# A two-block transformer kernel: the order of the tiles in the last feed-forward round before the second mixer

## The reference

```python
f_lat = sqrelu_mlp(modulate(h_lat, g_pre_ff[0], ml[3], ml[4]), w_ff1[0], w_ff2[0])
h_lat = h_lat + ml[5] * rms_norm_2(f_lat, g_post_ff[0])
f_ctx = sqrelu_mlp(modulate(h_ctx, g_pre_ff[0], mc[3], mc[4]), w_ff1[0], w_ff2[0])
h_ctx = h_ctx + mc[5] * rms_norm_2(f_ctx, g_post_ff[0])
...
u_lat = modulate(h_lat, g_pre_mix[1], ml[0], ml[1])      # layer 1
u_ctx = modulate(h_ctx, g_pre_mix[1], mc[0], mc[1])
p_ctx, p_lat = u_ctx @ w_in, u_lat @ w_in                # odd_mixer
```

## Time and profile before

| | us |
|---|---|
| median of 3 runs | 2056.38 |
| lowest and highest | 2055.04, 2061.04 |
| the profiled execution | 2060.76 |
| its span | 2058.9 |
| the last round's start to the first latent product of `proj1_k` | 63.84 |

### The profile page before, as it was taken

The page is one execution under the profiler, slowest core; times in us unless marked ns, Lnnn a source line. Parts: engine busy times, 40 slices in busy tenths (PEclk is TensorE's granted clock), DMA queues, the critical chain, the costliest instruction groups (busy, mean ns, idle before and its releaser), DMA issues. The chain is left out here.

```text
span 2058.9 us, 36819 instructions
## 1 busy us (share of the span) xinstructions
PE 1926.6 (94%) x15696; PEld 1615.2 (78%) x15696; DVE 1132.2 (55%) x1798; ACT 863.8 (42%) x1531; POOL 210.3 (10%) x249
## 2 busy tenths in 40 slices
PE   7998999899899999989999998999999879888998
PEld 5756998685699978856898987888877678677987
DVE  6554775465567655466556665544444545536643
ACT  5353664345456543445322334322222243545532
POOL 1100221020012200101113311000000101000000
PEclk9987999999799999999999999999999989998999
DMA  7682665458456552335000032333323214014653
GB/s 261 203 307 83 187 184 192 141 177 307 142 144 185 178 169 86 99 109 183 3 24 4 4 124 62 114 110 95 113 84 100 62 63 138 25 43 134 190 186 123
DMA packets 231641, 264.53 MB, mean 128 GB/s; under 512 B 14214, under 2 KB 153782, under 8 KB 231095
## 3 DMA queue, kind: packets, MB, share of 16 engines
q1 hardware_dynamic: 230891, 261.36, 40.1%
q10 hardware_dynamic: 588, 0.82, 0.1%
HBM read 261.07 MB, written 1.09 MB: 127 GB/s over the span
## 5 line engine op out<-in xcount | busy, mean ns | idle before, releaser
L401 PE MATMUL acc<-rounded,rounded 128*128 128x512 f32 (+1 forms) x2552 | 883.8, 346 | 24.7 <-DVE rounded L653 11.0
L402 PE MATMUL acc<-rounded,rounded 128*128 128x512 f32 (+1 forms) x2552 | 874.9, 343 | 0.0
L403 PE MATMUL acc<-rounded,rounded 128*128 128x512 f32 (+1 forms) x2552 | 874.1, 342 | 0.0
L385 DVE TENSOR_TENSOR rounded<-arena,rounded 128x2048 fp32r<-128x2048 f32 (+1 forms) x194 | 434.2, 2242 | 299.4 <-ACT rounded L374 299.3
L401 PEld LDWEIGHTS acc<-rounded,rounded 128*128 128x128 f32 x2552 | 488.0, 191 | 93.8 <-issue 20.5
L402 PEld LDWEIGHTS acc<-rounded,rounded 128*128 128x128 f32 x2552 | 488.1, 191 | 60.4 <-issue 1.9
L403 PEld LDWEIGHTS acc<-rounded,rounded 128*128 128x128 f32 x2552 | 487.5, 191 | 60.4
L374 ACT ACTIVATE rounded<-arena 128x2048 fp32r<-128x2048 f32 (+1 forms) x194 | 363.0, 1874 | 349.4 <-PE acc L403 308.4
L1406 DVE SCALAR_TENSOR_TENSOR arena<-acc,pcol,arena 128x254 f32<-128x254 f32 (+1 forms) x176 | 76.8, 478 | 52.3 <-ACT arena L1387 50.8
L823 PEld LDWEIGHTS sc<-arena 128*128 128x128 f32 x592 | 72.8, 196 | 37.9 <-ACT arena L929 20.4
L1990 PE MATMUL sc<-arena 64*64 64x64 f32 x2560 | 95.6, 224 | 6.9 <-DVE arena L2140 5.8
(11 more groups left out here) (243 smaller groups left out, 1691.8 us busy)
## 6 DMA issues: line engine op xcount, KB each, us to landing
arena<-in_w_ff SPq DMA_DIRECT2D x64, 1024.0 KB, 5.3
arena<-in_w_ada SPq DMA_DIRECT2D x48, 1024.0 KB, 5.2
arena<-in_w_up SPq DMA_DIRECT2D x88, 512.0 KB, 5.1
arena<-in_w_in SPq DMA_DIRECT2D x24, 1024.0 KB, 5.2
arena<-in_w_down SPq DMA_DIRECT2D x20, 1024.0 KB, 5.1
arena<-in_w_out SPq DMA_DIRECT2D x16, 1024.0 KB, 5.1
arena<-in_w_in_even SPq DMA_DIRECT2D x9, 1024.0 KB, 5.4
arena<-in_w_in_odd SPq DMA_DIRECT2D x8, 1024.0 KB, 5.3
```

What stands on the lines that cost most here:

```text
L385: dve.tensor_tensor(r32(w), w, r32(high_slot(c)[:, 0:size(c)]), ALU.subtract).then_inc(split_made, 1)
L401: pe.matmul(ps, ah, bh, start=first, stop=False)
L402: pe.matmul(ps, ah, bl, start=False, stop=False)
L403: return pe.matmul(ps, al, bh, start=False, stop=last)
```

## The change

The last round gets an order of its own, in the list `CONTEXT_FIRST` of (half, tile): (0, 0), (0, 1), (1, 0), (1, 1), (0, 2), (0, 3), (1, 2), (1, 3). So both halves of the two context tiles come first. `last_round` on PE, `add_last` on DVE and `round_squares` on ACT follow it.

- PE: the four small products stand ahead of the first four accumulators. Context tile 0 is transposed ahead of accumulator 6 (half 1 of tile 2), context tile 1 ahead of accumulator 7. In `proj1_k` both latent tiles are transposed ahead of context product 3.
- The second tile of both norms goes to the "sc" banks instead of "tr" (`TWO_POOLS`).
- DVE: the gate products of half 0 come after accumulators 1 (context) and 5 (latent); context tiles are finished after accumulators 2 and 3; `norm_scale` of context tile 0 after accumulator 4, of tile 1 after 5; `norm_low` of tile 0 after 5, of tile 1 after 6, ahead of the finish of latent tile 2. The split of the second `proj1_k` chunk moves from the middle of the round to its end, on DVE and ACT.
- ACT: `norm_high` of the context tiles moves in between the squares of accumulators 5, 6 and 7.
- The first weight chunk of the round is released after accumulator 6 instead of 4. The scratch of ACT's squares moves from `uT[1]`, which the norm now fills meanwhile, to a free part of `hid[1]`.
- POOL makes the second context tile's 1/rms ahead of the latent tiles' steps.

```diff
@@ plan
+            if e == EIGHTHS - 1:
+                release[-2] = (acc_full, acc_at[("ff2", e)] + 6)
...
+        CONTEXT_FIRST = [(0, 0), (0, 1), (1, 0), (1, 1), (0, 2), (0, 3), (1, 2), (1, 3)]
+        stage("near", sc=8)
         plan_norm(("mix", 1, 1))
         plan_norm(("mix", 1, 0))
-        stage("near", sc=8)
...
         def norm_fill(key, tt, half):
-            return tr_at[("norm", key)] + 2 * tt + half
+            if key in TWO_POOLS and tt:
+                return TWO_POOLS[key], {"acc": acc_at, "sc": sc_at}[TWO_POOLS[key]][("norm", key)] + half
+            return "tr", tr_at[("norm", key)] + 2 * tt + half
@@ DVE, in place of add_round's last round
+            def add_last(self, dve, key, following):
+                self.gate_wait(dve)
+                for n, (hf, t) in enumerate(self.order):
+                    if n < 4:
+                        near_dve(dve, 1, n)
+                    f = acc_at[key] + n
+                    o = self.o[:, t, hf * 512:(hf + 1) * 512]
+                    dve.tensor_tensor(o, o, filled(dve, "acc", f)[:, :], ALU.add).then_inc(drain("acc", f), 1)
+                    if n == 4:
+                        near_used(dve)
+                        norm_scale(dve, following, 0)
+                    if n in (1, 5):
+                        for x in (t - 1, t):
+                            self.squared(dve, 0, x)
+                            self.gate_half(dve, 0, x)
+                    if n == 5:
+                        norm_scale(dve, following, 1)
+                        for half in range(2):
+                            norm_low(dve, following, 0, half)
+                    if n == 6:
+                        for half in range(2):
+                            norm_low(dve, following, 1, half)
+                    if hf:
+                        self.finish(dve, t)
+                ahead_dve(dve, chunk_at[key] + HIGH)
@@ ACT, round_squares
-                tok_walk(act, ahead_act, last, ET, 2, squares, last=False)
+                for n, (hf, t) in enumerate(self.order):
+                    if n in (4, 5):
+                        norm_square(act, following, n - 4)
+                    wait_drained(act, "acc", acc_at[last] + n)
+                    cols = slice(hf * 512, (hf + 1) * 512)
+                    self.square(act, hf, t, self.o[:, t, cols], self.squares[:, t, :])
+                    if n == 5:
+                        norm_high(act, following, 0)
+                    if n == 6:
+                        norm_high(act, following, 1)
+                ahead_act(act, chunk_at[last] + HIGH)
@@ PE
-                    if block == 1 and n == 3 and key == ("ff2", EIGHTHS - 1):
-                        norm_turn(pe, ("mix", 1, 1), 0)
+            def last_round(key, lhsT):
+                for n, (hf, t) in enumerate(CONTEXT_FIRST):
+                    if n < 4:
+                        near_pe(pe, 1, n)
+                    if n >= 6:
+                        norm_turn(pe, ("mix", 1, 1), n - 6)
+                    w = parts(pe, chunk_at[key] + hf)
+                    ps = claim(pe, "acc", acc_at[key] + n)
+                    for k in range(ET):
+                        ins = mm3(pe, ps[:, :], lhsT(k, t), both(w, lambda v: v[:, k, :]), k == 0, k == ET - 1)
+                    ins.then_inc(acc_full, 1)
...
-            norm_turn(pe, ("mix", 1, 1), 1)
-            feat_gemm_by_stream(pe, "proj1_k", PK, 4, lambda s: ("mix", 1, s), {2: 0, 3: 1})
+            feat_gemm_by_stream(pe, "proj1_k", PK, 4, lambda s: ("mix", 1, s), {3: [0, 1]})
@@ POOL, post_pool
-                if norms and t >= 2:
+                if norms and t >= 2 and not (context_first and t == 3):
                     norm_pool(pool, tiles[t - 2][0], [tiles[t - 2][1]])
+                if context_first and t == 2:
+                    norm_pool(pool, *[(key, [tt]) for key, tt in tiles][1])
                 post.pool_rstd(pool, t)
```

More of the change, by code:

```diff
@@ L663, in norm_dve @@
                     norm_scale(dve, norm, 0)
-                if not norm[4]:
+                early = not norm[4] and norm[0] not in TWO_POOLS
+                if early:
                     norm_low(dve, norm, 0, 0)
@@ L669, in norm_dve @@
                     for half in range(2):
-                        if norm[4] or tt or half:
+                        if not early or tt or half:
                             norm_low(dve, norm, tt, half)
@@ L723, in feat_gemm_by_stream @@
                 for i in range(n):
[L724 to L725 removed]
+                    for tt in turns.get(i, ()) if s else ():
+                        norm_turn(pe, norm(0), tt)
                     w = parts(pe, chunk_at[key] + i // 2)
@@ L2371, in __init__ @@
                 self.ss, self.ms, self.rs = stats(2 * n), stats(n), stats(n)
+                self.order = CONTEXT_FIRST if key == "ff0" else [(hf, t) for hf in range(2) for t in range(n)]
                 self.rows_before = sum(len(p.streams) for p in posts.values())
```

91 lines of the change are left out of this document (40 added, 51 removed).

## The result

| | before | after |
|---|---|---|
| median of 20 runs each | 2059.05 | 2047.00 |
| lowest and highest | 2055.01, 2064.53 | 2041.76, 2060.84 |
| the profiled execution, its span | 2060.76, 2058.9 | 2041.76, 2039.9 |
| the last round's start | 1613.09 | 1607.18 |
| from there to the first latent product of `proj1_k` | 63.84 | 50.88 |

After to before is 0.9948, 95% interval 0.9936 to 0.9959: some 10.7 us faster, with 8.4 to 13.2 us in the interval. The ratio is not that of the two medians, which differ by 12.05 us. The forecast was 2043.6, range 2039.5 to 2050.0.

What follows compares the result with a forecast made beforehand. TensorE, busy 94%, was taken as the bound, waiting 8.0, 5.8 and 3.5 us for VectorE's serial chain. Work 42.2, waits 8.5 and joints 0.3 gave 51.0 against 63.84 us, so 2056.38 - 12.8 = 2043.6 us, range 2039.5 to 2050.0.

Steps and rivals of the forecast that it cites:

- The walk: Last round's start to proj1_k's first latent product, followed instruction by instruction: 51.0 us against 63.84, 12.8 less; chance 0.55.
- the slow 7.52 us of products 0 and 1: Context products 0 and 1 of proj1_k charged at the fallen clock, after a forecast wait of 3.4 us.
- The 'sc' banks are long empty, which takes away the 5.8 us.: Ahead of context tile 1's transposes: the 5.8 us wait for an emptied "tr" bank goes.
- Context product 2 waits 1.6 us for it.: In proj1_k: TensorE waits 1.6 us for the second chunk's split, now behind both latent tiles on VectorE.
- What lies behind moves as a whole.: Behind the first latent product: nothing changes length, the 2.64 us wait stays, changed releases cost nothing.
- the last gap of the stretch: Rival: clock also falls in the 2.6 us wait ahead of the first latent product, costing 1.8 us, 2045.4 us; chance 0.15.
- The queue: Rival: VectorE's queue from 1628 to 1664 is longer than walked, gain 8 us, 2048.4 us; chance 0.12.
- The waits did not shrink further: Rival: the 1.6 and part of the 2.6 and 3.4 us waits go, gain 16 us, 2040.4 us; chance 0.07.
- Slow from the first wait on: Rival: clock stays low from the first wait to the projections' end, 12.6 us slower, 2069.0 us; chance 0.03.
- Taken back behind: Rival: a wait behind proj1_k, a load in first place, swallows the gain, 2052 to 2058 us; chance 0.08.
- A gain in the stretch that the span does not show: Sign of a wrong forecast: round start to first latent product gets shorter, the whole execution does not.
- The base: Starting median of the whole kernel, 2056.38 us from three runs, minus 12.8 gives 2043.6 us.

Runs made afterwards that it cites:

- one_pool: Changed kernel with both tiles of each norm transposed through the "tr" banks again, no "sc" banks: ratio to before 0.9946, round start to first latent product 50.86 us.
- lows_last: Changed kernel with both context tiles' low and high parts behind the finish of all four tiles again: ratio to before 0.9989, round start to first latent product 56.66 us.
- old_tile_order: Changed kernel with the old tile order and context update, scale and transpose places; pools and late split kept: ratio to before 1.0017, round start to first latent product 60.19 us.
- filler: Changed kernel with 20 spare matmuls on TensorE ahead of context product 0 of proj1_k: ratio to before 0.9974, round start to first latent product 53.40 us.
- latent_scaled_first: Changed kernel with latent tile 0 scaled ahead of the second chunk's split, tile 1 behind it, latent transposes apart: ratio to before 0.9951, stretch 49.66 us.
- before_again: The kernel before, unedited, run once more for its trace: median 2055.33 us, round start to first latent product 64.04 us.
- split_mid: Changed kernel with the second proj1_k chunk's split moved between the two latent tiles: ratio to before 0.9953, round start to first latent product 49.76 us.
- combined: Changed kernel with split between latent tiles, latent transposes apart, latent tile 0 scaled between latent updates, tile 1 inside tile 0's low parts: ratio to before 0.9917, stretch 48.04 us.
- after_again: The changed kernel, unedited, run once more: median 2049.49 us, ratio to before 0.9949, round start to first latent product 50.87 us.

## Why the prediction was right, and where it was not

**The walk.** Forecast and measured, counted from the round's start:

| | forecast | measured |
|---|---|---|
| first transposes (wait) | 21.1 (0.9) | 21.12 (0.78) |
| first product of `proj1_k` (wait) | 31.9 (3.4) | 31.56 (2.87) |
| products 0 and 1 | 7.52 | 7.43 |
| context product 2 (wait) | 41.0 (1.6) | 40.70 (1.71) |
| first latent product (wait) | 51.0 (2.6) | 50.88 (2.50) |

No start is off by more than 0.4 us and no wait by more than 0.53. Following the chain through VectorE instruction by instruction was what made this possible: sums of TensorE's waits would not have given it, as one_pool shows. lows_last and old_tile_order came out within the stretches expected of them by the same kind of walk. One term of the sum was right in size and free in effect: the slow 7.52 us of products 0 and 1. filler made them fast, and product 2 started 40.72 us behind the round's start all the same.

**"The 'sc' banks are long empty, which takes away the 5.8 us."** Right that the wait goes, wrong why: one_pool has no second pool and the same stretch. The prediction's own walk had already put the gain of context tile 0 ahead of the latent tiles; the pool then had nothing left to free.

**"Context product 2 waits 1.6 us for it."** The wait was forecast to 0.1 us, and it was a cost, as the prediction had it: moving the split brought 1.1 us. The walk took 0.3 us for GpSimd's adds, and the one beside the split took 1.95. That this did no harm was not foreseen: tile 0 waited for product 2 in any case. In latent_scaled_first, where it does not, a slow add of this kind cost 0.87 us.

**"What lies behind moves as a whole."** The 2.64 us wait was there and no load or release came late. But of three traces of after two have a tail 3 us longer at a lower clock; lows_last and old_tile_order 10 and 13.5 us. This is the step that failed, in part. The ratio gives 10.7 us where the stretch gives 13.0; a tail that is 3 us longer in most executions of after and in few of before would make up the difference. That is argued: two and three traces can't set how often, and the interval of the ratio (8.4 to 13.2 us) holds the 13.0 as well, so that the medians don't show that anything is missing.

**The rivals.** The clock did not fall in the last gap of the stretch in any trace of after (2.50 us). The Trainium skill (TensorE: Matmul & The Clock Gate, "HAM oscillation") tells of a clock that falls in every wait between bursts of matmuls, with waits of about 3 to 5 us. The rows agree for the waits of 3.23 and 3.33 us; most waits here are shorter than the skill's. The 3.49 us wait of before, which the prediction took as its example, says nothing of this: the clock was already low ahead of it, as the eight transposes between the 5.80 us wait and this one show, with 2.32 us in place of 1.04:

```profile
1655.94 2.32 PE L611 MATMUL tr<-keep,arena 128*128 128x128 f32 x8 [5.80 <-DVE arena L648]
```

Behind 2.87 us it fell each time. Behind the 2.64 us ahead of the tail it fell in nine traces of thirteen (not in before, before_again, after and split_mid). Behind 2.49 us it fell in filler, lows_last and old_tile_order, and behind 2.50 us in no trace of after. Behind 2.11 us it fell in one_pool, and behind 2.09 us it did not in split_mid. So between 2.1 and 2.7 us both happen, and the length alone doesn't decide. The first 4 us behind the 2.11 us in one_pool:

```profile
1641.27:1645.27 4.00, 4.00 (x22) 4.00 (x23) 3.01 (x5) 0.44 (x1) 0.93 (x1) 0.60 0.68 234
```

The queue was as long as walked. The waits did not shrink further by themselves; combined reached the 3 us of that rival by other moves. "Slow from the first wait on" did not come: the one patch in the stretch was below 4 us long. "Taken back behind" was right in kind, by way of the clock and not of a load, and smaller than priced. "A gain in the stretch that the span does not show", named as a sign of error, is what lows_last and old_tile_order do: 7.2 and 3.7 us of gain in the stretch, of which the ratio shows 2.3 us in the one and in the other a loss of 3.5 (both intervals hold 1).

**The base.** The forecast subtracted from the median of three runs, 2056.38; that of twenty is 2059.05. With it the forecast would have been 2046.3, against 2047.0 measured.

## What to carry to other kernels

When one engine waits for another's serial chain, walk the chain and not the waits: taking one wait away can merely move it to the next place (the second pool, the spare matmuls), and it gains where something on the chain stood behind that wait (the split in the middle). Compare the stretch that was changed and the identical code behind it apart from each other, as a lower clock behind can take part of a gain, or all of it. A large instruction that is moved should be looked at for what runs beside it on the other engines, down to the smallest, and the traces should tell whether what got slower is on the path: the same slow add cost nothing in one kernel and 0.87 us in another.

## What the runs showed of the hardware

- **A tiny GpSimd operation beside a large VectorE one.** The add of L601 on 128x1 took 0.22 us at most places, and 1.95 and 2.23 us where it began 0.41 and 0.14 us after VectorE's split (2.28 and 2.29 us, both inputs in SBUF); each ended about 0.08 us after the split did. The power of L603 took 0.57 us, and 1.44 where it began within an update of VectorE (1.29 us), in before, after and split_mid alike; it then ended about 0.43 us after the update. The Trainium skill (SBUF — State Buffer, "Who interferes with whom") says that VectorE and GpSimd share a port that a VectorE instruction with two SBUF inputs holds for itself. The rows agree.
- **Short waits and the clock.** Behind a single wait of 2.1 to 3.4 us a patch at 1.2 GHz was mostly 3.4 us long and cost about 1.7 us (7.43 us for 48 matmuls that take 5.7 at the full clock). It began between 0.4 us before and 1.2 us after work resumed. What decides whether one follows a wait of 2.1 to 2.7 us stays open.
- **The tail.** The same 2080 matmuls of the same code took from 367.6 to 381.2 us, by what lay ahead of them or by the execution. after_again, lows_last and old_tile_order all end the tail's own wait of 2.19 us, about 60 us in, 1.5 us later than after does. Behind it, up to 110 us in, the clock was low for about 7 us in before and after, 10.5 in after_again, and in two pieces for 24 in lows_last and 31 in old_tile_order. The products of L837 then start 2.8, 10.7 and 13.9 us later than in after (90.5 us in): the whole difference is there by then. In old_tile_order the clock was down even 80 us behind the wait that the tail is counted from, and in before_again it was not (20 us of each, first old_tile_order, columns as above):

```profile
1767.81:1787.81 20.00, 20.00 (x86) 14.52 (x88) 6.42 (x18) 7.98 (x19) 0.00 (x0) 0.57 0.00 0
```
```profile
1765.76:1785.76 20.00, 17.47 (x140) 14.94 (x140) 7.74 (x22) 10.73 (x26) 0.00 (x0) 1.00 0.00 1
```
The 20.00 and 17.47 us of PE there are 86 and 140 matmuls. What carries the lower clock that far was not found.
